# A decoder layer on eight cores: when the second feed-forward block is normalised, when three weights are loaded, and how buffer addresses are chosen

## The chip, the cores and the metric

The kernel runs on the 8 cores of one Trainium2 chip. Each core takes one sequence of the batch and runs the same program; nothing is exchanged between cores. The time of a run is that of the slowest core, in microseconds (us) of device time. Times inside the kernel come from one profiled execution, on core 1, the slowest one, unless another core is named.

## The reference, cut to what matters

```python
x = x + g1 * rmsnorm(concat([y_mla, y_ret]) @ w_out, post_norm_mix)      # (B, S, 1024)
h = rmsnorm(x, pre_norm_ffn) * (1.0 + sc2) + sh2
f = (jax.nn.silu(h @ w_gate) * (h @ w_up)) @ w_down                       # D_FF = 2816
x = x + g2 * rmsnorm(f, post_norm_ffn)
```

S is 4096. `y_mla` is causal softmax attention over 8 heads (query and key width 96, value width 64) and `y_ret` is a chunked retention over 4 heads; both come out of one input projection of a normalised `x`. The change touches the feed-forward part (the last three lines) and the place where it meets the attention part.

## The kernel before, in words

A core's 4096 tokens are cut into 8 blocks of 512. The program has three stages.

1. **Input projection and retention**, for token blocks 0 to 7 (about 100 to 455 us).
2. **Attention**, over query blocks in the order 6, 7, 5, 4, 3, 2, 1, 0 (`order`; about 480 to 1090 us). Per query block it runs score matmuls into banks of PSUM, the exponential on ACT (the tile `PT`), the causal mask on POOL for tiles on the diagonal, and `PT` times `V` on PE. Into these loops other work is mixed as "fill": the queries of the next block, and `outproj` of the block before (L1122). `outproj` has a part `pre` per 128 tokens (loads `yg` and the residual `xt`, transposes) and a part `proj`: 16 matmuls with `Wo`, copies to `mo`, bn statistics, one `-0.5` power on POOL, `xt + mo` on POOL, and a store of `xt` to a scratch in HBM (`x_scr` in the rows, `x1` in the code).
3. **Feed-forward**, over the same 8 blocks in the same order (L1370 on). For each block `prep2` (L1231) loads four tiles `xa` of 128 tokens from the scratch, squares them on ACT with a running sum, takes the power on POOL, scales them on DVE into `xn`, transposes them on PE and writes the result, scaled and shifted, to `h2T` on DVE. Then come 22 steps `jj`: 8 matmuls with a slice of `Wg`, 8 with one of `Wu`, SiLU on ACT into a tile `sgt`, and `up * sgt` on DVE into `h1T`. Then, for each of the four rows of 128 tokens (`j`), 2 x 22 matmuls with `Wd` into two banks, squares on ACT (`t`), the power on POOL, a scaling on DVE, `xb + t` on POOL and the store to `out`.

In the first feed-forward block (`si == 0`) the `outproj` of the last query block (`late`, L1373) is mixed between the steps `jj`, and at `jj == 10` stands `prep2` of the second block. In the later blocks `prep2` of the next block stands at `jj == 10` too.

The weights are read once, cast to bf16 on the way, by transfers issued on POOL: `Wg` and `Wu` in six groups each (five of 512 columns, the sixth of 256), `Wd` in six groups. `loads[si]` (L1224) names the groups whose transfers stand at the head of query block `si`; `tail_loads` (L1225) names those after the last query block; `Wd3` to `Wd5` stand at `jj == 9` of the first feed-forward block. Everything else is loaded and stored by SP.

**What sets the order.** `record` writes all operations down in program order with what they read and write. `_list_schedule` (L344) then lays them out per engine by a list schedule with modelled durations; where several operations are ready, the one written down first goes first. The result is a fixed order on each engine, and each engine works strictly in its order. A transfer is issued by its engine and lands later.

**What sets the addresses.** A first pass records the life of each buffer in program order; `_place` (L281) then gives each an address, and a buffer may lie where another lay before it. The new buffer's first writer waits then for the old one's last readers. `place` (L274) tries seeds (random changes in the order in which long-lived buffers are placed) and takes the first plan that fits.

Of the kernel before, what the change touches and what calls it, by code (L numbers as in the profile page):

```python
# [19 lines left out]
NSB = 8  # L20
# [142 lines left out]
class Sched:  # L163
    def __init__(self, plan=None):
        self.order = []
        self.plan = plan
        self.bufs = []
        self.arena = None
        self.nc = None

    def buf(self, name, cols, dt=F32, pin=False, fix=None):
        size = cols * (2 if dt == BF16 else 4)
        size = (size + 63) // 64 * 64
        b = Buf(name, size, "sb")
# [6 lines left out]
        if self.plan is not None:  # L181
            b.addr, b.over = self.plan[b.no]
        if self.plan is None:
            v = self.arena[:, 0:size // 4]
            if dt != F32:
                v = v.bitcast(dt)
            b.v = v[:, 0:cols]
        else:
            b.v = self.nc.alloc_sbuf_tensor_at(name, [128, cols], dt, offset=BASE + b.addr)[:, :]
# [84 lines left out]
    def place(self):  # L274
        for seed in range(200):
            plan = self._place(seed)
            if isinstance(plan, list):
                return plan
        raise RuntimeError(plan)

    def _place(self, seed):  # L281
# [8 lines left out]
        def cls(b):  # L290
            if b.pin or b.fix is not None:
                return -1 if b.fix is not None else 0
            return 1 if b.last - b.first > 1000 else 2

# [4 lines left out]
        for i, b in enumerate(order):  # L299
# [21 lines left out]
            best = None  # L321
            for lo, hi in holes:
# [9 lines left out]
                if best is None or sc < best:  # L332
                    best = sc
# [171 lines left out]
def record(nc, S, dr, arena, psum):  # L505
# [717 lines left out]

    loads = [[], [], [('g', 0), ('u', 0), ('g', 1)], [('u', 1)], [('g', 2), ('u', 2)], [('g', 3)], [], [('u', 3)]]  # L1224
    tail_loads = [('g', 4), ('u', 4), ('g', 5), ('u', 5), ('d', 0), ('d', 1), ('d', 2)]  # L1225

# [144 lines left out]
    for si, s in enumerate(order):  # L1371
        nxt = []
        late = outproj(order[-1], yms[NSB - 1]) if si == 0 else []  # L1373
        for jj in range(NJ):
# [15 lines left out]
            if si == 0 and jj == 9:  # L1390
                ffn_load([('d', 3), ('d', 4), ('d', 5)])
            if jj == 10 and si + 1 < NSB:
                for _ in prep2(order[si + 1], (0, 1) if si else (4, 5), nxt):
                    pass
        for j in range(4):
# [17 lines left out]
            for hf in range(2):  # L1413
                hs = slice(hf * 512, (hf + 1) * 512)
                stt(t_.v[:, hs], PS[fb[hf]], st.v[:, 2:3], G2b.v[:, hs], ALU.mult, ALU.mult, [PSB[fb[hf]], (st, 2), G2b], [(t_, hf)])
                tt("pool", xt.v[:, hs], xt.v[:, hs], t_.v[:, hs], ALU.add, [(xt, hf), (t_, hf)], [(xt, hf)])
            dma("sp", dr["out"][tb * 128:(tb + 1) * 128, :], xt.v, r=[xt], w=[(outD, tb)])
        h2T = nxt[0] if nxt else None
    OP("sp", lambda g: None, r=[outD])


def build_nc():
# [37 lines left out]
    with contextlib.ExitStack() as ctx:  # L1460
# [6 lines left out]
        record(nc, S0, dr, arena, psum)  # L1467
        S = Sched(S0.place())
        record(nc, S, dr, arena, psum)
# [97 lines left out]
```

How the kernel before makes its waits and increments, by code:

```python
    def then_inc(self, *a, **kw):  # L144
        return self
# [326 lines left out]
        def run(e, engobj):  # L472
            for op in self.ops[e]:
                for d in op.waits:
                    if d.is_dma:
                        n = NSEM[d.eng]
                        engobj.wait_ge(dsem[d.eng][d.dma_i % n], 16 * (d.dma_i // n + 1))
                    else:
                        engobj.wait_ge(esem[d.eng], d.count)
                ins = op.emit(engobj)
                if op.is_dma:
                    ins.then_inc(dsem[e][op.dma_i % NSEM[e]], 16)
                elif op.marked:
                    if ins is None:
                        ins = engobj.nop()
                    ins.then_inc(esem[e], 1)
```

## Time and profile before

| | us |
|---|---|
| median of three runs | 2189.97 |
| lowest and highest of them | 2080.72, 2330.53 |
| the profiled execution | 2075.85 |
| its span, from the first to the last instruction of core 1 | 2074.0 |
| spans of the eight cores | 2057.9 to 2074.0 |
| PE busy (matmul) | 1873.1 (90%) |
| DVE, ACT, POOL busy | 812.3, 959.3, 623.7 |
| read and written in HBM | 172 MB, 49 MB |

PE, DVE, ACT, POOL and SP are the engines; PEld is PE's loading of weights, which overlaps the matmuls. "bank" is a bank of PSUM. A number in square brackets at the end of a row of a timeline is how long the engine was idle before the row, and the name behind the arrow is what ended that wait. `x4` is the number of instructions merged in a row.

### The profile page before, as it was taken

The numbers are of one execution on the slowest core, as the hardware profiler recorded it, in microseconds if no ns is written. First come the engines' busy times: TensorE is split into PE (matmuls) and PEld (weight loads), VectorE is DVE, ScalarE is ACT, GpSimd is POOL, SyncE is SP. The second block draws the span as 40 slices with busy tenths as digits, with TensorE's granted clock in tenths as the row PEclk, the third lists the DMA queues.
The fourth block names the chain that finished last, engine by engine and source line by source line (L and its number), as shares of the span: only waits on it lengthen the run. The fifth ranks groups of instructions, "written<-read, shape, count | busy, mean of one in ns | idle before, by whom it ended". The sixth has DMA issues, their size and how long they took to land.

```text
span 2074.0 us, 39088 instructions; the slowest of 8 cores (2057.9 to 2074.0 us)
## 1 busy us (share of the span) xinstructions
PE 1873.1 (90%) x13536; PEld 973.7 (47%) x13536; DVE 812.3 (39%) x1739; ACT 959.3 (46%) x1485; POOL 623.7 (30%) x919
## 2 busy tenths in 40 slices
PE   0598999768889899999989799999999999999998
PEld 0255545434455555555544344444444444444443
DVE  3356556454354233456685422222131313122121
ACT  3466656528889999998851112121121212121111
POOL 3345456440243233335573411030201112020202
PEclk9999999988999999999999999999999999999999
DMA  7924445444333252354379812030201112030101
GB/s 227 190 60 128 124 122 130 122 82 148 86 111 95 61 104 85 83 126 115 106 181 176 216 42 82 21 102 11 91 30 63 53 51 72 21 102 21 51 21 62
DMA packets 94665, 195.51 MB, mean 94 GB/s; under 512 B 10376, under 2 KB 40584, under 8 KB 94472
## 3 DMA queue, kind: packets, MB, share of 16 engines
q1 hardware_dynamic: 65560, 162.79, 25.0%
q0 software_dynamic: 28912, 30.21, 10.0%
q8 instruction: 113, 1.85, 0.4%
q14 instruction: 80, 0.66, 0.1%
HBM read 172.32 MB, written 48.76 MB: 107 GB/s over the span
## 4 chain that ended last, share of the span: by engine, by line
PE 74%; DMA 8%; ACT 6%; issue 4%; SPq 3%; DVE 3%; POOL 2%; POOLq 0%; DVEq 0%; ACTq 0%
PE bank L542 72%; ACT PT L518 5%; SPq L515 3%; PE bank L549 2%; DMA W<-w 2%; DMA yg_scr<-yn 2%; DMA waf<-w_ada 1%; DMA x_scr<-xt 1%; DMA ckTb<-ck_scr 1%; DMA xa<-x_scr 1%; DVE Q L534 1%; DVE mo L529 1%; ACT yn L518 0%; DMA gp<-gpost 0%; POOL yn L521 0%
## 5 line engine op out<-in xcount | busy, mean ns | idle before, releaser
L518 ACT ACTIVATE PT<-bank 128x1024 bf16<-128x1024 f32 (+3 forms) x584 | 515.3, 944 | 75.7 <-PE bank L542 68.5
L542 PE MATMUL bank<-h2T,Wg 128*128 128x512 bf16 x1408 | 336.9, 383 | 14.3 <-ACT sgt L518 11.4
L542 PE MATMUL bank<-Q,KT 96*128 96x512 bf16 (+3 forms) x1152 | 319.9, 365 | 28.8 <-ACT PT L518 16.0
L542 PE MATMUL bank<-h2T,Wu 128*128 128x512 bf16 x1408 | 333.5, 380 | 2.0 <-DVE bag L1172 2.0
L518 ACT ACTIVATE sgt<-bank 128x512 bf16<-128x512 f32 x176 | 104.9, 597 | 477.7 <-PE bank L542 441.3
L542 PE MATMUL bank<-Wd,h1T 128*128 128x512 bf16 x1408 | 307.2, 379 | 0.0
L521 DVE TENSOR_TENSOR h1T<-bank,sgt 128x512 bf16<-128x512 f32 x176 | 121.5, 691 | 425.9 <-PE bank L542 415.9
L542 PE MATMUL bank<-W,hT 128*128 128x512 bf16 (+2 forms) x1280 | 259.6, 358 | 27.8 <-DMA W<-w 9.6
L542 PEld LDWEIGHTS bank<-V,PT 128*128 128x128 bf16 x4224 | 201.3, 97 | 124.5 <-issue 15.2
L542 PE MATMUL bank<-V,PT 128*128 128x65 bf16 x4224 | 222.4, 193 | 4.5 <-POOL PT L521 3.2
L542 PEld LDWEIGHTS bank<-h2T,Wg 128*128 128x128 bf16 x1408 | 138.1, 98 | 181.6 <-issue 20.5
L542 PEld LDWEIGHTS bank<-Wd,h1T 128*128 128x128 bf16 x1408 | 137.8, 98 | 166.1
L542 PEld LDWEIGHTS bank<-h2T,Wu 128*128 128x128 bf16 x1408 | 137.6, 98 | 166.6 <-issue 3.0
L521 POOL TENSOR_TENSOR st<-st 128x1 f32<-128x1 f32 x32 | 6.2, 193 | 644.8 <-ACT t L518 644.8
L542 PEld LDWEIGHTS bank<-W,hT 128*128 128x128 bf16 x1280 | 123.8, 100 | 144.3 <-issue 42.0
L518 ACT ACTIVATE t<-bank 128x512 f32<-128x512 f32 x64 | 38.1, 596 | 280.6 <-PE bank L542 240.7
L542 PE MATMUL bank<-Wo,yT 128*128 128x512 bf16 x512 | 155.6, 379 | 3.3 <-DVE bag L1172 1.9
L521 POOL TENSOR_TENSOR PT<-PT,trib 128x256 bf16<-128x256 bf16 x136 | 88.5, 670 | 220.4 <-ACT PT L518 219.9
L542 PEld LDWEIGHTS bank<-Q,KT 96*128 96x128 bf16 x1152 | 93.6, 97 | 112.9 <-issue 75.1
L529 DVE SCALAR_TENSOR_TENSOR t<-bank,st,G2b 128x512 f32<-128x512 f32 x64 | 45.1, 747 | 254.6 <-POOL st L521 254.6
L521 POOL TENSOR_TENSOR xt<-xt,mo 128x512 f32<-128x512 f32 x64 | 87.6, 1385 | 31.1 <-DVE mo L529 26.1
L521 POOL TENSOR_TENSOR xb<-xb,t 128x512 f32<-128x512 f32 x64 | 79.6, 1265 | 29.7 <-DVE t L529 29.3
(159 smaller groups left out, 1857.6 us busy)
## 6 DMA issues: line engine op xcount, KB each, us to landing
xt<-x SPq DMA_DIRECT2D x64, 512.0 KB, 5.4
x_scr<-xt SPq DMA_DIRECT2D x32, 512.0 KB, 2.7
xa<-x_scr SPq DMA_DIRECT2D x32, 512.0 KB, 6.2
xb<-x_scr SPq DMA_DIRECT2D x32, 512.0 KB, 3.3
out<-xb SPq DMA_DIRECT2D x32, 512.0 KB, 2.6
waf<-w_ada SPq DMA_DIRECT2D x4, 2048.0 KB, 22.6
wadab<-w_ada POOLq DMA_DIRECT2D x8, 1024.0 KB, 14.1
yg_scr<-yn SPq DMA_DIRECT2D x32, 256.0 KB, 3.3
```

The lines of the kernel that those rows point to most:

```text
L515: return OP(q, lambda g: g.dma_start(out=out, in_=in_), r, w, dma=True)
L518: return OP("act", lambda g: g.activation(out=out, in_=in_, func=func, **kw), r, w)
L521: return OP(eng, lambda g: g.tensor_tensor(out=out, in0=a, in1=b, op=op), r, w)
L529: return OP("dve", lambda g: g.scalar_tensor_tensor(out=out, in0=a, scalar=sc, in1=b, op0=op0, op1=op1), r, w)
L534: return OP(eng, lambda g: g.tensor_copy(out=out, in_=a), r, w)
L542: x = g.matmul(out, lhsT=l, rhs=rh, start=st, stop=sp, **kw)
L549: x = g.transpose(out=out, in_=i, identity=identb.v)
```

## The change

It has three parts.

- `prep2` of the second feed-forward block leaves `jj == 10` of the first block and is written behind the first row (`j == 0`) of that block's down projection. It takes banks 0 and 1 there for its transposes, where it took 4 and 5. The later blocks keep theirs.
- The transfers of `Wg5`, `Wu5` and `Wd0` are written at the head of the last query block and no longer behind it.
- Of the seeds, the first eight plans that fit are each recorded and laid out by the list schedule, and the one with the smallest modelled end is taken. The limit of life by which `_place` calls a buffer long-lived varies with the seed.

```diff
     def place(self):
-        for seed in range(200):
+        for seed in range(400):
             plan = self._place(seed)
             if isinstance(plan, list):
-                return plan
-        raise RuntimeError(plan)
+                yield plan
...
-            return 1 if b.last - b.first > 1000 else 2
+            return 1 if b.last - b.first > (1000, 500, 1500, 250)[seed % 4] else 2
...
-    loads = [[], [], [('g', 0), ('u', 0), ('g', 1)], [('u', 1)], [('g', 2), ('u', 2)], [('g', 3)], [], [('u', 3)]]
-    tail_loads = [('g', 4), ('u', 4), ('g', 5), ('u', 5), ('d', 0), ('d', 1), ('d', 2)]
+    loads = [[], [], [('g', 0), ('u', 0), ('g', 1)], [('u', 1)], [('g', 2), ('u', 2)], [('g', 3)], [], [('u', 3), ('g', 5), ('u', 5), ('d', 0)]]
+    tail_loads = [('g', 4), ('u', 4), ('d', 1), ('d', 2)]
...
-            if jj == 10 and si + 1 < NSB:
-                for _ in prep2(order[si + 1], (0, 1) if si else (4, 5), nxt):
+            if jj == 10 and 0 < si < NSB - 1:
+                for _ in prep2(order[si + 1], (0, 1), nxt):
                     pass
...
             dma("sp", dr["out"][tb * 128:(tb + 1) * 128, :], xt.v, r=[xt], w=[(outD, tb)])
+            if si == 0 and j == 0:
+                for _ in prep2(order[1], (0, 1), nxt):
+                    pass
...
-        S = Sched(S0.place())
+        best = None
+        for plan in itertools.islice(S0.place(), 8):
+            S = Sched(plan)
+            S.dry = True
+            record(nc, S, dr, arena, psum)
+            S.schedule()
+            if best is None or S.model_time < best[0]:
+                best = S.model_time, plan
+        S = Sched(best[1])
```

The numbers behind names in the following rows are those of the buffers, and line numbers after the change are one higher than before. ACT, in the first feed-forward block, before (`xn<-xa` are the squares of `prep2`, `t` those of the down projection):

```order
L518 ACTIVATE sgt<-bank 128x512 x9
L518 ACTIVATE xn_806,xst_928<-xa 128x1024
L518 ACTIVATE xn_806,xst_932<-xa 128x1024
L518 ACTIVATE xn_806,xst_934<-xa 128x1024
L518 ACTIVATE sgt<-bank 128x512 x3
L518 ACTIVATE xn_806,xst_930<-xa 128x1024
L518 ACTIVATE sgt<-bank 128x512 x9
L518 ACTIVATE t_948,st_947<-bank 128x512 x2
```

The same place after:

```order
L519 ACTIVATE sgt<-bank 128x512 x17
L519 ACTIVATE xn_806,xst_944<-xa 128x1024
L519 ACTIVATE sgt<-bank 128x512
L519 ACTIVATE xn_806,xst_942<-xa 128x1024
L519 ACTIVATE sgt<-bank 128x512
L519 ACTIVATE xn_806,xst_946<-xa 128x1024
L519 ACTIVATE sgt<-bank 128x512 x2
L519 ACTIVATE t_940,st_939<-bank 128x512 x2
L519 ACTIVATE t_951,st_950<-bank 128x512 x2
L519 ACTIVATE xn_806,xst_948<-xa 128x1024
```

The first square has moved from behind the 10th of the block's 22 SiLU to behind the 18th, and the fourth stands behind the squares of two rows of the down projection.

PE, the place of the transposes of the second block's `xn`, before (in the last steps `jj` of the first block):

```order
L542 MATMUL bank<-h2T_807,Wg_894 128x512 x8
L549 MATMUL bank<-identb,xn_806 128x128 x16
L542 MATMUL bank<-h2T_807,Wu_903 128x512 x8
L549 MATMUL bank<-identb,xn_806 128x128 x16
L542 MATMUL bank<-h2T_807,Wg_904 128x512 x8
```

and after (behind 130 of the 176 matmuls of the down projection; `Wd_906` is `Wd0`, `Wd_924` is `Wd4`, `Wd_925` is `Wd5`):

```order
L543 MATMUL bank<-Wd_923,h1T 128x512 x4
L543 MATMUL bank<-Wd_925,h1T 128x512 x2
L543 MATMUL bank<-Wd_924,h1T 128x512 x4
L550 MATMUL bank<-identb,xn_806 128x128 x16
L543 MATMUL bank<-Wd_925,h1T 128x512 x2
L543 MATMUL bank<-Wd_906,h1T 128x512 x4
L550 MATMUL bank<-identb,xn_806 128x128 x8
L543 MATMUL bank<-Wd_909,h1T 128x512 x4
L550 MATMUL bank<-identb,xn_806 128x128 x8
```

The 32 transposes have moved by some 210 matmuls (88 that stood between them and the down projection, and 130 of its own). The last lines show as well that the rows of the down projection are no longer worked off one by one on PE.

POOL, the issues of the last three `Wd` and what stands between them, before (`Wd_923`, `Wd_924`, `Wd_925` are `Wd3`, `Wd4`, `Wd5`):

```order
L515 DMA Wd_923<-wd 128x4x1024
L515 DMA Wd_924<-wd 128x4x1024
L521 TENSOR_TENSOR xt_868<-xt_868,mo_874 128x512 x2
L526 TENSOR_SCALAR xst_934<-xst_934 128x1
L521 TENSOR_TENSOR xst_934<-xst_934,mhalf 128x1
L521 TENSOR_TENSOR bag_879<-bag_879,e_890 128x1
L521 TENSOR_TENSOR bag_879<-bag_879,mhalf 128x1
L521 TENSOR_TENSOR xt_872<-xt_872,mo_877 128x512 x2
L515 DMA Wd_925<-wd 128x2x1024
```

and after:

```order
L516 DMA Wd_923<-wd 128x4x1024
L516 DMA Wd_925<-wd 128x2x1024
L522 TENSOR_TENSOR bag_879<-bag_879,e_890 128x1
L522 TENSOR_TENSOR bag_879<-bag_879,mhalf 128x1
L522 TENSOR_TENSOR xt_872<-xt_872,mo_877 128x512 x2
L527 TENSOR_SCALAR xst_944<-xst_944 128x1
L522 TENSOR_TENSOR xst_944<-xst_944,mhalf 128x1
L527 TENSOR_SCALAR xst_942<-xst_942 128x1
L522 TENSOR_TENSOR xst_942<-xst_942,mhalf 128x1
L527 TENSOR_SCALAR xst_946<-xst_946 128x1
L516 DMA Wd_924<-wd 128x4x1024
```

`Wd4` (four chunks) and `Wd5` (two) have changed places: in the new plan `Wd4` lies where `xt_872` and `mo_877` lay, so its transfer waits until the last store of `xt` to the scratch has landed.

## Rows read from the trace of the kernel before

**Rows 1.** Span and granted clock of the slowest core:

```profile
core 1: 2074.0 us, clock 0.978
```

**Rows 2.** Busy time by stage, core 1 (stretch, length, busy and count of each engine, clock, DMA):

```profile
100.00:455.00 355.00, 318.55 (x2318) 179.07 (x2317) 204.35 (x608) 207.73 (x437) 180.09 (x295) 0.98 0.43 110
455.00:480.00 25.00, 6.41 (x15) 1.51 (x14) 4.74 (x15) 6.73 (x12) 4.04 (x5) 0.50 0.84 204
480.00:1080.00 600.00, 552.29 (x6262) 330.15 (x6259) 301.10 (x623) 522.06 (x607) 223.03 (x299) 0.98 0.39 103
1080.00:1220.00 140.00, 120.07 (x622) 56.02 (x623) 71.73 (x139) 24.79 (x40) 48.38 (x63) 0.94 0.73 169
1220.00:2074.00 854.00, 845.12 (x4058) 388.82 (x4056) 190.43 (x290) 161.19 (x330) 131.78 (x208) 1.00 0.16 53
...
1190.00:1200.00 10.00, 6.69 (x31) 3.61 (x32) 4.54 (x8) 3.20 (x6) 0.74 (x2) 0.55 0.23 58
```

**Rows 3.** What PE waited for, 1082 to 1225 us, core 1 (total, times, longest):

```profile
PE bank L542 <- ACT sgt L518: 11.4, 2, 8.9
PE bank L542 <- DVE bag L1172: 3.9, 3, 2.0
PE bank L542 <- DVE h2T L526: 2.9, 1, 2.9
```

**Rows 4.** The same on core 7:

```profile
PE bank L542 <- ACT sgt L518: 14.9, 2, 11.9
```

**Rows 5.** Timeline of PE, end of the first feed-forward block's steps `jj` (start, length, what):

```profile
1170.04 1.89 PE L542 MATMUL bank<-h2T,Wg 128*128 128x512 bf16 x8 [2.46 <-ACT sgt L518]
1173.92 2.54 PE L542 MATMUL bank<-h2T,Wu 128*128 128x512 bf16 x8 [1.99 <-DVE bag L1172]
1176.25 2.97 PE L542 MATMUL bank<-h2T,Wg 128*128 128x512 bf16 x8
...
1193.31 3.57 PE L542 MATMUL bank<-h2T,Wg 128*128 128x512 bf16 x8 [8.91 <-ACT sgt L518]
1196.68 1.91 PE L549 MATMUL bank<-identb,xn 128*128 128x128 bf16 x16
...
1200.37 1.06 PE L549 MATMUL bank<-identb,xn 128*128 128x128 bf16 x16
...
1218.53 38.15 PE L542 MATMUL bank<-Wd,h1T 128*128 128x512 bf16 x176
```

**Rows 6.** Timeline of ACT at the same place:

```profile
1164.36 1.06 ACT L518 ACTIVATE xn<-xa 128x1024 bf16<-128x1024 f32 x1 [15.09 <-DMA xa<-x_scr]
...
1189.77 1.06 ACT L518 ACTIVATE xn<-xa 128x1024 bf16<-128x1024 f32 x1 [9.86 <-DMA xa<-x_scr]
...
1192.57 1.69 ACT L518 ACTIVATE sgt<-bank 128x512 bf16<-128x512 f32 x3 [1.65 <-DMA x_scr<-xt]
```

**Rows 7.** Chain of waits, the two last stores of `xt` (start, length until landed):

```profile
1173.32 9.62 DMA x_scr<-xt
...
1183.48 8.89 DMA x_scr<-xt
```

**Rows 8.** Timeline of POOL, the last residual addition:

```profile
1180.48 2.48 POOL L521 TENSOR_TENSOR xt<-xt,mo 128x512 f32<-128x512 f32 x2 [4.97 <-DMA xt<-x]
```

**Rows 9.** Tile `Wd`, issues and landing of its six transfers:

```profile
L515 POOL DMA_DIRECT2D Wd<-wd x6: 744/788/835, 1099.0 to 1183.6; - x6
...
DMA to landing us min/median/max: 9.2/19.7/37.1
```

**Rows 10.** Tile `Wu`, its three transfers between 700 and 1000 us:

```profile
DMA to landing us min/median/max: 9.5/11.4/11.9
```

**Rows 11.** Timeline of SP, the first store of the feed-forward output:

```profile
1234.30 0.34 SPq L515 DMA_DIRECT2D out<-xb  x1
```

**Rows 12.** Tile `xa` of the first feed-forward block's normalisation, 1030 to 1082 us:

```profile
DMA to landing us min/median/max: 4.1/4.1/5.4
```

**Rows 13.** Tile `xa` of the second block's normalisation, 1100 to 1220 us:

```profile
DMA to landing us min/median/max: 5.1/6.1/6.7
```

More of the change, by code:

```diff
@@ L2 @@
 import heapq
+import itertools
 import types
@@ L169, in __init__ @@
         self.nc = None
+        self.dry = False
     def buf(self, name, cols, dt=F32, pin=False, fix=None):
@@ L182, in buf @@
             b.addr, b.over = self.plan[b.no]
-        if self.plan is None:
+        if self.plan is None or self.dry:
             v = self.arena[:, 0:size // 4]
```

## The prediction, made before the changed kernel ran

> **What bounds the kernel now.** I read the busy time by stage first [rows 2]. From 1220 us on PE is busy 845.1 of 854 us: the feed-forward part is bound by PE, and the 8.9 us missing are the end of the last block. The input projection leaves PE idle for 355 - 318.6 = 36.4 us, the change to attention for 18.6 us of 25, attention for 600 - 552.3 = 47.7 us, and the stretch from 1080 to 1220 us, which holds the steps `jj` of the first feed-forward block, for 19.9 us. The reader is to see that the two written edits can act only in the last of these and just ahead of it: everything behind is full.
>
> The waits of PE in that stretch come next [rows 3]: 11.4 us for ACT's SiLU, in two waits; core 7 has the same with 14.9 us [rows 4], so it is no accident of one core. The timeline of PE gives the places [rows 5]: 2.46 us before 1170.04, 1.99 us before 1173.92, and 8.91 us before 1193.31. The timeline of ACT says why [rows 6]. ACT works in its order, and at 1149 us the next thing there is the square of a tile `xa` of `prep2`; ACT stands idle for 15.1 us until its load has landed, and the SiLU behind it stands too. The fourth square waits for a second time, 9.9 us, until 1189.77. Its load lies where a tile `xt` lay, whose store was issued at 1173.32 and took 9.62 us [rows 7]. The SiLU behind it waits another 1.65 us for the last store of `xt` (1183.48 + 8.89 = 1192.4), since its tile `sgt` lies on that buffer [rows 6, 7]. PE has three pairs of banks to run ahead in; they are used up, so it stands.
>
> **The change part by part.** All sums are against the profiled execution, 2075.85 us (span 2074.0 [rows 1] and 1.85 us around it). The lowest of the three runs shown is 4.9 us above it, their median 114 us; the number I give is on the scale of the profiled execution.
>
> *`prep2` moved behind the first row of the down projection.* What it takes away:
>
> - The wait of 8.91 us. In the new order the first 18 of the 22 SiLU stand ahead of any square, and in the new plan none of the last ones lies on a buffer whose store is late. I take all of it.
> - The wait of 2.46 us: ACT was held up by the third square. All of it.
> - The wait of 1.99 us: DVE came to the product for `h1T` late, behind copies and statistics of `outproj`, which stay. Between 0 and 1.99; I take 1.0.
> - The slow clock behind these gaps. The granted clock of 1190 to 1200 us is 0.55 [rows 2], that is, PE was for most of it on its level of 1.2 GHz in place of 2.4 GHz, after it had stood for 8.9 us. Eight matmuls take 1.89 us at the upper level and 2.54, 2.97 and 3.57 us behind the gaps, and 16 transposes 1.91 in place of 1.06 us [rows 5]: 0.65 + 1.08 + 1.68 + 0.85 = 4.3 us. I take it all.
>
> Together 8.9 + 2.5 + 1.0 + 4.3 = 16.7 us. The 32 transposes (2 x 0.89 us of PE) cost the same in either place. So the down projection, which began at 1218.5, should begin near 1218.5 - 16.7 - 1.8 = 1200.
>
> What it adds is a deadline in the down projection. Three of the loads of `xa` can go early, but the fourth lies on the tile `t` of the first row, and stands on SP behind that row's store to `out`. That store was issued 1234.30 - 1218.53 = 15.8 us after the down projection began, when the row's 44 matmuls ended at 9.5 us [rows 5, 11]. Now both halves of the row end after 48 matmuls (10.4 us at 0.217 us each, 38.15 / 176), so the store goes at 16.7 and the load at 17. It lands 4.1 to 6.7 us later [rows 12, 13], the square takes 1.06 us [rows 6], and I put 2 us on the two small steps on POOL and the scaling on DVE: ready at 24 to 27 us. The transposes stand behind 130 matmuls, at 28.2 us. Hidden, with 1 to 4 us to spare; where the load takes the 9.6 us of a slow transfer [rows 7], PE waits 2 us. Value 0, bounds 0 and 3. What covers it is the down projection itself.
>
> *The order of the last `Wd`.* `Wd4` now lies on the last `xt` and can be issued only when the store of it has landed, and it stands on POOL ahead of the statistics of `prep2`. The last `xt + mo` waited for its load until 1180.48 [rows 8], and its store was issued at 1183.48 and landed at 1192.4 [rows 7]. PE's last matmuls with `Wo` come about 5 us later in the new order (three groups of 8 stand in between), which the wait of 4.97 us for the load [rows 8] about swallows. So `Wd4` is issued near 1193. PE wants it after 36 matmuls of the down projection, at 1200 + 7.8 = 1207.8. A transfer of that size lands after 9.5 to 11.9 us where little else moves [rows 10], and six `Wd` took 9.2 to 37.1 us, median 19.7, when they were issued in a heap [rows 9]. That gives 1203 to 1213: between no wait and 5 us, with 2 or 3 us of slow clock on top. Only three tiles `xa` move beside it, so it is nearer to the first rows: I take 1.0, bounds 0 and 8.
>
> A page of the Trainium skill prices such a transfer: by "DMA: Bandwidth & Descriptors", Anatomy of one DMA, it takes about 2.0 us plus its bytes at 436 GB/s, an estimate of 4.4 us for the 1 MB written here. This trace has 9.5 us at the least for it, so the trace disagrees and decides; by the page this term would be 0 and the forecast 1 us lower.
>
> *`Wg5`, `Wu5` and `Wd0` released with the last query block.* PE waits for no weight in the stretch [rows 3], so an earlier landing gives nothing by itself. In the order of POOL two more transfers now stand between the masks of that query block: 0.8 us each [rows 9], 0 to 1.6, I take 1.0. They also share the DMA engines with the four loads of `xa` for the first block, at whose end PE already waits 2.9 us for `h2T` [rows 3]. The same loads took 4.1 us in the median there and 6.1 us where `Wd3` and `Wd4` were under way [rows 12, 13]: 2.0 us later at most for one load; I take 1.3.
>
> *The plan.* Other addresses give other waits in every stage. They remove no work. The idle time they can move is the 36.4, 18.6 and 47.7 us ahead of 1080 us [rows 2]; a tenth of these 103 us in either direction is what I allow. I take 0, bounds -10 and +10. That a plan is picked by modelled time is no price: the model holds fixed durations and no contention.
>
> **Sum.** -16.7 + 0 + 1.0 + 1.0 + 1.3 + 0 = -13.4 us. 2075.85 - 13.4 = 2062 us, 0.6% faster.
>
> **The rivals.**
>
> 1. *The stall moves to the new deadlines.* `Wd4` late by 5 us and slow clock (8 us), and the fourth `xa` late (3 us): 16.7 - 11 - 2.3 = 3 us gained, 2072 us. For it: the landing of up to 37 us [rows 9] and POOL standing in front of `Wd4`. Against it: few transfers are left at that time.
> 2. *The early weight transfers hold up the first normalisation: slower than before.* 3 MB are read in f32 and written as half of that in the 30 us in which the four `xa` of the first block, the residuals and `yg` come in. If a load of `xa` had to wait for the whole of them, PE would stand at its first feed-forward matmul for what they take: two of them at 9.5 to 11.9 us [rows 10] are 19 to 24 us, and 3 to 4 us of slow clock. At 2062 that is 2083 to 2089; I put it at 2085. It decides from a delay of 13.4 us on. Against it: `xa` beside two `Wd` under way took only 2 us longer [rows 12, 13].
> 3. *The plan gives more, or takes more, than the edits.* With a tenth of the idle time the sum ends at 2052 or at 2072.
> 4. *Nothing happens.* The new plan puts a late `sgt` or `xa` on a late buffer again and another wait of 8.9 us comes back: 2074 us.
>
> A rule of the skill bears on the second. "DMA: Bandwidth & Descriptors", SWDGE vs HWDGE vs iDMA, says that transfers issued from POOL and those issued from SP feed different queues inside each DMA engine, and that the engine takes turns between them. By that a load of `xa` is at most about doubled and never waits for a whole weight; the trace's step from 4.1 to 6.1 us agrees with it, and by it the rival could not reach its deciding point.
>
> **How the numbers follow.** The forecast's own case, 2056 to 2068 us, has 0.55. Rival 1 has 0.15, the plan's gain 0.10 (2046 to 2056), its loss 0.08 (2068 to 2078), nothing 0.07, the slower rival 0.05. The range is to hold 8 in 10: from 2049, which cuts off about half of the plan's gain, to 2076, which takes in rivals 1 and 4 and most of the plan's loss. A difference of 2%, some 41 us, is about what a measurement of this kernel can tell from no change. To be faster by that much the kernel would have to lose twice what the whole stretch from 1080 to 1220 us holds in idle time: 0.02. To be slower by it needs the second rival twice over: 0.03. Within it: 0.95.
>
> **What would show the steps right or wrong.** In the profile after: no wait of PE for `sgt` above 2 us between 1080 and 1220, and the down projection's first matmul at 1197 to 1204; a granted clock of 1.00 in the slices around it; `Wd4` landing before the 37th matmul of the down projection; the transposes with `xn` inside the down projection without a gap in front; PE's wait for `h2T` near 1082 us at 2.9 to 5 us; the stages up to 1080 us of the same length within 10 us. A gap of PE behind the first 36 matmuls with `Wd` would show rival 1; a gap of 10 us before the first matmul with `Wg` rival 2. The prediction would be wrong altogether if the projection or the attention stage changed by more than those 10 us.

## The result: 0.5% faster, and where the time went

The changed kernel takes 2073.62 us in the median of 20 runs (lowest 2064.64), the kernel before 2085.94 us in the median of its 20 (lowest 2078.25). The ratio is 0.9949, with a 95% interval of 0.9931 to 0.9967: about 10.6 us faster. That is inside the 2% called "no change". The profiled execution takes 2070.42 us. The two medians are over all 20 runs; the ratios and intervals of this document leave out the runs in which the cores of a die run at a lower clock, and without them the medians are about 2072 and 2083.5 us.

How to read the profile after: on core 1 the first matmul with `Wg` is at 1082.2 us, where it was at 1082.7 before, so that the two traces of this core can be laid side by side from there. Spans and clock of two cores (core 0 is the slowest now):

```profile
core 0: 2068.9 us, clock 0.977
core 1: 2058.9 us, clock 0.978
```

Busy time by stage, core 1 (stretch, length, busy and count of PE, PEld, DVE, ACT and POOL, granted clock, DMA share, GB/s):

```profile
100.00:455.00 355.00, 314.91 (x2259) 176.18 (x2258) 197.33 (x596) 203.77 (x428) 177.59 (x290) 0.95 0.42 105
480.00:1080.00 600.00, 548.09 (x6246) 325.74 (x6244) 301.59 (x621) 518.74 (x602) 223.41 (x298) 0.99 0.40 106
1080.00:1220.00 140.00, 134.32 (x691) 61.91 (x690) 69.43 (x133) 26.88 (x48) 50.38 (x66) 0.98 0.64 160
...
1060.00:1070.00 10.00, 7.78 (x49) 3.79 (x48) 7.71 (x21) 3.95 (x8) 9.78 (x17) 0.83 1.08 210
1070.00:1080.00 10.00, 6.09 (x62) 4.10 (x60) 10.00 (x20) 1.74 (x5) 6.21 (x9) 0.76 0.80 176
1080.00:1090.00 10.00, 8.33 (x57) 4.03 (x56) 5.60 (x12) 5.43 (x8) 6.07 (x8) 0.72 0.64 214
1190.00:1200.00 10.00, 10.00 (x48) 4.51 (x46) 3.46 (x5) 5.40 (x10) 3.04 (x7) 1.00 0.76 224
```

From 1080 to 1220 us PE is now idle for 140 - 134.3 = 5.7 us, against 19.9 [rows 2], and the slice from 1190 us is full at clock 1.00, where it had 0.55. The waits of PE from 1082 to 1225 us show no `sgt` at all any more (total, times, longest):

```profile
PE bank L543 <- DVE bag L1173: 1.9, 2, 1.2
PE bank L543 <- ACT PT L519: 1.3, 2, 0.9
PE bank L550 <- DVE mo L535: 1.0, 2, 0.5
PE bank L543 <- DVE mo L535: 0.8, 1, 0.8
```

The timeline of PE of core 1, through the down projection of the first block, has no gap before the 37th matmul or before the transposes; it is to be read beside [rows 5]:

```profile
1196.37 1.89 PE L543 MATMUL bank<-h2T,Wg 128*128 128x512 bf16 x8
1198.10 1.89 PE L543 MATMUL bank<-h2T,Wu 128*128 128x512 bf16 x8
1199.82 28.22 PE L543 MATMUL bank<-Wd,h1T 128*128 128x512 bf16 x130
1227.88 1.06 PE L550 MATMUL bank<-identb,xn 128*128 128x128 bf16 x16
1228.77 1.46 PE L543 MATMUL bank<-Wd,h1T 128*128 128x512 bf16 x6
```

**A table for all that follows.** The cores enter the feed-forward part 16 us apart before and 21 us apart in the changed kernel (29 in e7), and a single span hides a difference of 5 us. So I cut each core's trace at the same matmuls and average the lengths over the eight cores. "Projection" goes from the first projection matmul to the first `V` times `PT`; "q 6 to 2" is the first six query blocks; "last two" goes from the first `V` times `PT` of query block 1 to the first matmul with `Wg`; "q 1 to PE's end" from the same start to PE's last matmul, and "PE idle" is what PE stands still in it; "tail" is from there to the end of the span. The modelled end is the planner's. "Last two" does not hold the same matmuls in every kernel, since the list schedule also puts attention matmuls behind the first `Wg`: 494 before and in e1, 486 in the changed kernel, 498 in e12, 501 in e2, but 472 in e11 and 458 in e4 and e5 (all matmuls of PE in the stretch, core 1). So between e4, e5 or e11 and the others only the stretch to PE's end is a fair comparison. The stretches from query block 7 on repeat within about 1 us from core to core, save those with a late load in them. The projection does not: its mean was 417.8, 418.6 and 424.7 us in e1, e7 and e12, which have the same addresses there. (For e12 there were too few runs for a ratio.)

| kernel | modelled end | projection | q 6 to 2 | last two | q 1 to PE's end | PE idle | tail | ratio (95%) |
|---|---|---|---|---|---|---|---|---|
| before | 1992.5 | 417.1 | 540.3 | 59.2 | 1041.5 | 29.5 | 8.9 | 1 |
| changed | 1982.8 | 418.9 | 538.4 | 65.6 | 1031.9 | 19.0 | 10.7 | 0.9949 (0.9931 to 0.9967) |
| e1 move alone | 1982.7 | 417.8 | 540.4 | 59.0 | 1024.2 | 14.3 | 8.9 | 0.9932 (0.9903 to 0.9961) |
| e2 loads alone | 1996.1 | 412.2 | 541.2 | 62.6 | 1040.7 | 26.7 | 9.6 | 0.9965 (0.9938 to 0.9992) |
| e4 choice alone | 1990.2 | 418.8 | 540.4 | 58.8 | 1029.5 | 19.5 | 9.4 | 0.9968 (0.9944 to 0.9991) |
| e5 changed, three transfers held | 1983.0 | 415.8 | 538.9 | 61.8 | 1029.7 | 18.1 | 10.6 | 0.9918 (0.9887 to 0.9949) |
| e6 changed, fewer waits | 1982.8 | 416.1 | 537.0 | 65.0 | 1031.4 | 19.3 | 8.8 | 0.9906 (0.9879 to 0.9933) |
| e7 move, fewer waits | 1982.7 | 418.6 | 537.3 | 58.9 | 1024.2 | 14.7 | 8.8 | 0.9875 (0.9847 to 0.9902) |
| e8 both edits, first plan | 1988.7 | 412.6 | 539.5 | 62.9 | 1032.2 | 20.7 | 9.3 | 0.9945 (0.9894 to 0.9997) |
| e9 changed without the move | 1988.1 | 425.5 | 539.5 | 67.4 | 1039.2 | 24.4 | 10.8 | 0.9989 (0.9962 to 1.0016) |
| e10 changed, worst plan of eight | 2000.1 | 429.3 | 544.6 | 64.4 | 1036.4 | 23.8 | 9.5 | 1.0051 (1.0031 to 1.0070) |
| e11 as e7, best plan of 400 | 1979.0 | 412.5 | 540.2 | 66.3 | 1032.1 | 19.3 | 8.8 | 0.9912 (0.9890 to 0.9934) |
| e12 as e1, two more transfers | 1982.9 | 424.7 | 541.9 | 64.2 | 1030.9 | 18.6 | 8.9 | none |

From the first row to the second the mean span falls from 2067.5 to 2059.9 us, 7.6 us: the stretch of the steps `jj` (first `Wg` to first `Wd`) from 135.7 to 117.9 us, -17.8; what follows it +1.8, since the transposes have moved there; the last two query blocks **+6.4**; the tail **+1.8**; query blocks 6 to 2 -1.9, projection +1.8 and the start +0.2. So the stall was removed as forecast, and half of it was paid back in two places. Of the 6.4 us, 3.6 are idle time of PE (9.6 before, 13.2 after) and 2.7 are longer busy time (49.7 and 52.4) with 8 matmuls fewer, at a lower clock: 0.83, 0.76 and 0.72 in the slices from 1060 us on core 1, where before it was

```profile
1060.00:1070.00 10.00, 9.30 (x65) 4.13 (x62) 9.90 (x26) 4.97 (x10) 9.10 (x15) 1.00 0.87 170
1070.00:1080.00 10.00, 6.77 (x73) 4.07 (x72) 10.00 (x20) 3.05 (x6) 9.80 (x16) 1.00 0.73 203
1080.00:1090.00 10.00, 7.31 (x45) 3.61 (x46) 6.23 (x13) 3.70 (x5) 4.89 (x5) 0.83 0.76 236
```

The waits of PE in the last two query blocks of the changed kernel, 1017 to 1082 us on core 1, lie at `PT` and `mo`, and hardly at `h2T`:

```profile
PE bank L543 <- ACT PT L519: 4.5, 9, 1.3
PE bank L550 <- DVE mo L535: 2.2, 2, 1.5
...
PE bank L543 <- DVE mo L535: 1.1, 2, 0.9
...
PE bank L550 <- DVE h2T L527: 1.1, 1, 1.1
```

The 7.6 us are from one execution of each kernel; the runs say 10.6. The experiments ask who pays for the 6.4 us.

### The profile page after: what moved, and what is told of

Read it like the earlier page. It is cut to its first block, busy times and chain, and to the rows that moved or that the text cites. A ratio compares the mean times of both kernels' runs of the same rounds, so it can differ in the third digit from the quotient of the medians.

```text
span 2068.9 us, 39095 instructions; the slowest of 8 cores (2047.6 to 2068.9 us)
## 1 busy us (share of the span) xinstructions
PE 1875.2 (91%) x13536; PEld 970.5 (47%) x13536; DVE 814.9 (39%) x1739; ACT 959.2 (46%) x1485; POOL 620.1 (30%) x919
## 4 chain that ended last, share of the span: by engine, by line
PE 73%; DMA 9%; ACT 7%; issue 4%; DVE 3%; SPq 2%; POOL 1%; POOLq 0%; DVEq 0%; ACTq 0%
PE bank L543 71%; ACT PT L519 5%; DMA yg_scr<-yn 3%; PE bank L550 2%; SPq L516 2%; DMA W<-w 2%; DMA waf<-w_ada 1%; DMA ckTb<-ck_scr 1%; ACT yn L519 1%; DVE Q L535 1%; DMA xa<-x_scr 0%; DVE mo L530 0%; DMA kp_scr<-kpT 0%; DMA wstage<-wkv 0%; ACT xn L519 0%
## 5 line engine op out<-in xcount | busy, mean ns | idle before, releaser
L543 PE MATMUL bank<-W,hT 128*128 128x512 bf16 (+2 forms) x1280 | 263.4, 361 | 44.3 <-DVE r L522 14.3
```

The lines of the kernel that those rows point to most:

```text
L543: x = g.matmul(out, lhsT=l, rhs=rh, start=st, stop=sp, **kw)
```

## The experiments

**The two edits and the choice, one at a time.** The first theory (L) was that the early weight transfers cost the 6.4 us, the second (P) that the chosen addresses do. e1 is the move alone:

```diff
-            if jj == 10 and si + 1 < NSB:
-                for _ in prep2(order[si + 1], (0, 1) if si else (4, 5), nxt):
+            if jj == 10 and 0 < si < NSB - 1:
+                for _ in prep2(order[si + 1], (0, 1), nxt):
...
+            if si == 0 and j == 0:
+                for _ in prep2(order[1], (0, 1), nxt):
+                    pass
```

> Kernel before with one edit: prep2 of the second block behind the first row of the down projection. Loads and plan rule as before. Measured by the mean over the eight cores of four stretches of PE: last two query blocks (first V times PT of query block 1 to the first matmul with Wg: 59.2 us before, 65.6 after), steps jj of the first block (to the first matmul with Wd: 135.7 and 117.9), rest (to PE's end: 846.6 and 848.4), tail (to the span's end: 8.9 and 10.7). Both theories: steps jj 118 to 120, rest 848.4. Theory L (the early weight transfers cost the 6.4 us of the last two query blocks): they stay at 59.2, tail 8.9 to 10.7, ratio 0.992 or 0.993. Theory P (the chosen plan costs them): 59.2 as well, since this kernel has the plan of before. If they rise to 65 here, it is the moved prep2 itself that costs them, ratio 0.996.

It gained 17.3 us from query block 1 on and left the last two query blocks and the tail as they were. To PE's end it takes 7.7 us less than the changed kernel; the ratios, 0.9932 and 0.9949, lie the same way, but their intervals overlap. So the move does not cost anything; what was paid back comes with the other parts, loads and plan. The expectation calls this "the plan of before". That holds up to the steps `jj` of the first feed-forward block only: from there on e1's `sgt` and `xa` have other addresses, and no `sgt` lies on the last `xt` any more, where one did [rows 6, 7]. The 17.3 us are thus order and addresses together.

e2 is the other edit alone:

```diff
-    loads = [[], [], [('g', 0), ('u', 0), ('g', 1)], [('u', 1)], [('g', 2), ('u', 2)], [('g', 3)], [], [('u', 3)]]
-    tail_loads = [('g', 4), ('u', 4), ('g', 5), ('u', 5), ('d', 0), ('d', 1), ('d', 2)]
+    loads = [[], [], [('g', 0), ('u', 0), ('g', 1)], [('u', 1)], [('g', 2), ('u', 2)], [('g', 3)], [], [('u', 3), ('g', 5), ('u', 5), ('d', 0)]]
+    tail_loads = [('g', 4), ('u', 4), ('d', 1), ('d', 2)]
```

> Kernel before with one edit: Wg5, Wu5 and Wd0 at the head of the last query block (the first plan that fits is then another). Theory L: last two query blocks 64 to 66 us against 59.2, all else as before, ratio 1.003. Theory P: 59 to 60 us and ratio 1.000. Both: the steps jj of the first block stay near 135.7, since an earlier weight ends no wait there; below 131 would mean that the crowd of transfers had a part in the late loads of xa, and the move had less to take away.

The last two query blocks rose to 62.6 us (with 7 matmuls more in them), and the steps `jj` fell to 131.4. That is half of what L said, and the ratio, 0.9965, lies below both forecasts. The addresses moved with the edit, so this run alone decides nothing, and whether `jj` fell by the addresses or by a smaller crowd of transfers stays open.

e4 is the third part alone, the choice among eight plans on the program of before:

```diff
-        S = Sched(S0.place())
+        best = None
+        for plan in itertools.islice(S0.place(), 8):
...
+            if best is None or S.model_time < best[0]:
+                best = S.model_time, plan
+        S = Sched(best[1])
```

> Kernel before with the choice among eight plans alone (modelled end 1990.2 us against 1992.5). Theory L and P: no more than 3 us either way, steps jj 133 to 137, ratio 0.999 to 1.001. If plans matter as much as theory P needs, the stretches ahead of the feed-forward part should differ from before by some us in sum: last two query blocks outside 58 to 61.

This missed: the steps `jj` took 124.0 us against 135.7, and the stretch to PE's end fell by **12.0 us** with not one operation moved by hand. The timeline of ACT of core 1 says how (the squares of the second block, their `READ_ACCUMULATOR` rows left out):

```profile
1157.17 1.06 ACT L519 ACTIVATE xn<-xa 128x1024 bf16<-128x1024 f32 x1 [12.73 <-DMA xa<-x_scr]
...
1161.87 1.06 ACT L519 ACTIVATE xn<-xa 128x1024 bf16<-128x1024 f32 x1 [3.55 <-DMA xa<-x_scr]
...
1173.63 1.06 ACT L519 ACTIVATE xn<-xa 128x1024 bf16<-128x1024 f32 x1 [5.62 <-DMA xa<-x_scr]
...
1178.27 1.05 ACT L519 ACTIVATE xn<-xa 128x1024 bf16<-128x1024 f32 x1
```

ACT still waits 12.73 us in front of the first square, as it did before [rows 6], but the wait of 9.86 us for a tile on the last `xt` but one has become 5.62, and PE waits 0.9 us for `sgt` where it waited 11.4 [rows 3] (2.5 us on core 7, where it was 14.9 [rows 4]). In this plan none of the second block's four `xa` and none of the block's `sgt` lies on an `xt` of `outproj`, and no SiLU waits for a store of `xt` any more. A plan brings its own order as well: ACT has two squares ahead of the next SiLU here, and three before [rows 6]. Addresses and the order that follows from them made most of the stall, though `prep2` stood at the same place.

e9 asks the same from the other side, the changed kernel with the move undone:

```diff
-            if jj == 10 and 0 < si < NSB - 1:
-                for _ in prep2(order[si + 1], (0, 1), nxt):
+            if jj == 10 and si + 1 < NSB:
+                for _ in prep2(order[si + 1], (0, 1) if si else (4, 5), nxt):
```

> The changed kernel with prep2 of the second block back at jj == 10; early loads and choice among plans stay (seed 20 is chosen again, modelled end 1988.1 us). If the move is worth here what it was worth in the plan of before, from query block 1 to PE's end takes 1031.9 + 17.3 = 1049 us. If the plan's addresses take most of the stall away by themselves, as the choice alone did (1041.5 to 1029.5), the move is worth only some 5 us: 1035 to 1039, ratio 0.996 to 0.999. Last two query blocks 64 to 66 in either case; tail 10 to 11, with 23 waits ahead of the last reduction.

1039.2 us, so the move is worth 7.3 us beside the choice, just above the 1035 to 1039 expected, and 17.3 without it. The last two query blocks, at 67.4 us, lay outside the 64 to 66. Move and choice remove the same waits, and their gains do not add: 17.3 + 12.0 would be 29.3.

**Early transfers or addresses?** Written out with the three transfers recorded behind the last query block, but with the changed kernel's addresses, the program comes out with the same order of instructions on all five engines, so there is no run of it. The list schedule issues a transfer as soon as its buffer is free in the model, wherever it is written: the kernel before issues `Wg5` at 1045.1 us too. The edit to `loads` acts only through the addresses, by making three buffers live longer. To hold the transfers back I had to make them wait for something:

```diff
+    for a_, kw_ in held:            # Wg5, Wu5, Wd0
+        dma(*a_, r=[yms[NSB - 1]], **kw_)
```

> The changed kernel with its own addresses, but the transfers of Wg5, Wu5 and Wd0 made to wait for the last head of the last query block, so that they are issued about 1095 to 1110 us and not at 1047 to 1058 us. From the first V times PT of query block 1 to PE's end the changed kernel takes 1031.9 us (mean of the cores), the one with the move alone 1024.2. Theory L (the transfers and their issues in the last query blocks cost it): 1024 to 1027, last two query blocks 59 to 61 against 65.6. Theory P (addresses and the order that follows from them): 1030 to 1034, last two 64 to 66.

The stretch to PE's end fell by 2.2 us, to 1029.7, between the two forecasts and close to P's 1030. The last two query blocks fell by 3.8, to 61.8, but with 28 matmuls fewer in them. The addresses are the changed kernel's; the order is not: from about 1040 us on the list schedule laid out all five engines otherwise (modelled end 1983.0 against 1982.8). Then the opposite, in e12: the move alone, which keeps its addresses, with the contents of `Wu5` and `Wd0` read and cast a second time behind the sixth head of query block 1:

```diff
+                    if si == 6 and h == 5:
...
+                            dma("pool", dr["spare"][i_, :, 0:c_ * n_].rearrange("p (c n) -> p c n", c=c_), src, r=[(ym, 5)], w=[S.key("spare")])
```

> The move alone, with the addresses it had, and two transfers more: the contents of Wu5 and Wd0 are read and cast a second time in the last part of query block 1, into a scratch in HBM that nobody reads, so that four weight transfers are issued in the last two query blocks, as in the changed kernel, and not two. Taking the three out of the changed kernel's last query blocks gave 3.8 us there (65.6 to 61.8) and 2.2 us to PE's end. If the transfers cost by themselves: last two query blocks 62 to 63 against 59.0, and from query block 1 to PE's end 1026 to 1028 against 1024.2. If all of it is addresses and order: 59 to 60 and 1024 to 1025. If transfers were the whole difference to the changed kernel: 65 to 66 and 1032.

The last two query blocks took 64.2 us and the stretch to PE's end 1030.9: **+6.7 us with two transfers more** (0.5 MB and 1 MB written), more than L's number and nearly as much as the difference to the changed kernel. Two things keep this from being the price of the transfers. They end in HBM and not in the core's own memory. And though the addresses are those of e1, the order is not: ACT's is the same, but PE, DVE, POOL and SP have another one from about 1050 us on (modelled end 1982.9 against 1982.7). No run changes the transfers and leaves the order. The loads of `xa` from query block 1 to the first matmul with `Wg`, from issue to landing, in e1 on core 3:

```profile
DMA to landing us min/median/max: 3.2/3.4/4.8
```

in the changed kernel on cores 1 and 6:

```profile
DMA to landing us min/median/max: 4.7/6.5/8.1
```

```profile
DMA to landing us min/median/max: 5.1/6.0/10.1
```

and in e12 on core 3:

```profile
DMA to landing us min/median/max: 3.4/5.5/13.6
```

On cores 0, 1, 3 and 6 the longest is 5.0 to 5.4 us before, 4.5 to 5.3 in e1, 7.9 to 10.1 in the changed kernel and 10.0 to 13.6 in e12; the medians differ by less, 3.4 to 5.2 in e1 and 4.5 to 6.6 in the two others. ACT takes these squares in order among the exponentials of the query block, so one late load can hold up attention as well; the fourth square of e12, on core 3:

```profile
1074.81 1.06 ACT L518 ACTIVATE xn<-xa 128x1024 bf16<-128x1024 f32 x1 [4.95 <-DMA xa<-x_scr]
```

The Trainium skill says in "DMA: Bandwidth & Descriptors", SWDGE vs HWDGE vs iDMA, that the DMA engines take turns between the queues fed by POOL and by SP. I had drawn from it that a load of `xa` beside a weight is at most about doubled. e12, with the addresses of e1, does not agree: the longest load takes 10.0 to 13.6 us against 4.5 to 5.3, 1.9 to 2.8 times as long on these four cores, with up to three weight transfers in flight, and the measurement decides.

One weight transfer is enough for a long load, and it matters which of the two is issued first. The fourth load of `xa` stands next to the transfer of `Wu3` in e1 and e5 alike; in e1 it is issued 0.5 us ahead of it (core 1),

```profile
1055.94 0.32 SPq L515 DMA_DIRECT2D xa<-x_scr  x1
1056.49 0.96 POOL L515 DMA_DIRECT2D Wu<-wu  x1
```

and in e5 2.3 us behind it:

```profile
1053.65 0.97 POOL L517 DMA_DIRECT2D Wu<-wu  x1 [0.50 <-issue]
1055.98 0.32 SPq L517 DMA_DIRECT2D xa<-x_scr  x1
```

Ahead of `Wu3`, by 0.5 to 0.8 us, this load takes 3.2 to 5.4 us on the eight cores of before and of e1; behind it, by 2.3 to 2.5 us, 7.3 to 9.2 us on the eight cores of e4 and of e5. So the long load of e5 does not stand there without a weight: holding three transfers back left `Wu3` in front of it. Nor is the longest landing the price by itself. PE's idle time in the last two query blocks (mean of the cores) is 11.9 us in e4, where the longest landing is 7.7 to 8.3 us, 13.2 in the changed kernel with 7.9 to 10.1, and only 10.9 in e12 with 8.8 to 13.6; it is 9.6 before and 9.0 in e1.

What remains with the transfers held (1029.7 against 1024.2 of e1, 5.5 us) comes with the plan and its order. One difference is seen on SP. In the changed kernel it issues two loads of `xa` just ahead of the four of `yg` (timeline of SP, core 1):

```profile
1036.07 0.99 SPq L516 DMA_DIRECT2D xa<-x_scr  x2
1037.25 8.53 SPq L516 DMA_DIRECT2D yg<-yg_scr  x4
```

where e1 issues one:

```profile
1038.43 0.51 SPq L515 DMA_DIRECT2D xa<-x_scr  x1
1039.10 6.94 SPq L515 DMA_DIRECT2D yg<-yg_scr  x4
```

DVE waits for that `yg`, 5.05 us in the changed kernel and 2.39 us in e1, and has the copies `mo` behind it, for which PE waits (DVE, then PE of the changed kernel, core 1):

```profile
1044.17 1.10 DVE L526 TENSOR_SCALAR ygb<-yg,sv 128x512 bf16<-128x512 f32 x2 [5.05 <-DMA yg<-yg_scr]
```

```profile
1047.31 0.38 PE L550 MATMUL bank<-identb,ym 128*128 128x128 bf16 x4 [1.55 <-DVE mo L535]
```

The load of `yg` was issued before the first weight transfer of that stretch, at 1046.8 us, and e5 has a wait of 2.10 us at the same transposes, so this part does not need the weights. It is some 1.5 us. The kernel before has a wait of 4.00 us for `yg` there too, with 59.2 us for the last two query blocks, so the wait of DVE by itself explains little. How the 7.7 us between e1 and the changed kernel divide stays open: holding the transfers gives 2.2, adding them to the other plan costs 6.7, and 5.5 are left with them held, each time with another order of the engines mixed in.

**Does the modelled end order plans?** e3 and e8 are one kernel, the two diffs of e1 and e2 with the first plan that fits; of e3 only the ratio is used, 0.9933 (0.9898 to 0.9968).

> The changed kernel without the choice among plans: both edits, first plan that fits (modelled end 1988.7 us, that of the chosen plan 1982.8). Theory L: last two query blocks 65.6 as in the changed kernel, ratio 0.995 to 0.997. Theory P: they return to 59 to 61, tail 8.9, ratio 0.992. By the modelled times it would be 5.9 us slower than the changed kernel, 0.998.

> Both edits with the first plan that fits, once more for an undisturbed profile. Theory L and P as for e3_both_first_plan: from query block 1 to PE's end 1032 by L and 1024 to 1027 by P (modelled end 5.9 us later than with the chosen plan: 1038). Last two query blocks 62.6 if they are as with the early loads alone, 65.6 if as in the changed kernel; tail 9 to 9.6.

1032.2 us to PE's end: the plan modelled 5.9 us later than the chosen one took as long. It fell where my first rival had put the danger in the changed kernel: PE waited for a late `Wd` in the down projection on all eight cores, for 0.4 to 5.6 us. The waits of PE from 1180 to 1260 us on core 7:

```profile
PE bank L542 <- DMA Wd<-wd: 5.6, 1, 5.6
```

e10 takes the plan of the eight with the latest modelled end:

```diff
-        for plan in itertools.islice(S0.place(), 8):
+        for plan in itertools.islice(S0.place(), 4, 5):
```

> The changed kernel with the fifth of the eight plans, the one with the latest modelled end (2000.1 us against 1982.8). If modelled time orders plans on the chip, query block 6 to PE's end takes 10 to 20 us more than the 1570.3 of the changed kernel, ratio 1.000 to 1.004. If it doesn't (the first plan, modelled 5.9 us later, took 1571.7), within 4 us of it, ratio 0.994 to 0.997. Tail near 9.3, since only 3 waits stand ahead of the last reduction.

and e11, on the kernel e7 (below), the one with the earliest among 400 seeds:

```diff
-        for seed in range(200):
+        for seed in (41,):
```

> The move alone with fewer waits, as e7, with the plan of the earliest modelled end among 400 seeds (1979.0 us against 1982.7). If modelled time orders plans: query block 6 to PE's end 1558 against 1561.5 in e7, ratio 0.985 to 0.986. If it doesn't: 1558 to 1568, ratio 0.987 to 0.990. For the projection there is no forecast by the model: 412 to 419.

The worst plan is worse, as forecast: 544.6 + 1036.4 = 1581.0 us from query block 6 to PE's end, against 1570.3, 10.7 us for a modelled 17.3; with its projection it is 0.5% slower than before. The best plan is not best: 540.2 + 1032.1 = 1572.3 us against 1561.5 of e7, 10.8 us more for a modelled 3.7 less. That is outside both forecasts (1558, and 1558 to 1568). It too has `Wu5` issued in the last query blocks. In these comparisons the model was right about a plan 17.3 us worse; modelled differences of 2.3 (e4), 3.7 (e11) and 5.9 us (e8) said nothing about the measured ones, -12.0, +10.8 and +0.3 us.

**The tail.** It grew from 8.9 to 10.7 us on every core alike. The end of POOL's timeline in the changed kernel, core 1:

```profile
2050.40 0.19 POOL L522 TENSOR_TENSOR st<-st 128x1 f32<-128x1 f32 x1 [3.98 <-issue]
```

ACT's last square had ended at 2048.98 us. "Issue" means that the profile shows nothing that the engine waited for. In between the trace has 22 semaphore instructions of POOL, 61 ns apart, from 2049.02 to 2050.29 us: the tile `st` lies in this plan where 21 transfers once wrote or read, and POOL, which has never asked for them, now asks for each. All had landed long ago. e6 changes the bookkeeping alone: an engine that waits for an operation takes over what that operation's engine knew of transfers.

```diff
+                known_dma[e] |= d.dmas
                 for f in ENGS:
...
             op.waits = waits
+            op.dmas = frozenset(known_dma[e])
```

> The changed kernel, same addresses and same order on every engine; an engine leaves out the wait for a transfer that it knows to have landed through another engine's earlier wait (7263 waits become 6228; the last reduction on POOL has 1 in place of 22). If the 1.3 us before that reduction are the one-by-one working off of these waits, the tail falls from 10.7 to 9.3 to 9.5 us. Theory that such waits are free everywhere else: from query block 1 to PE's end 1031 to 1032 as before, ratio 0.994. Theory that they hold the engines up in the attention part as well: two to six us less ahead of the feed-forward part, ratio 0.991 to 0.993.

The tail is 8.8 us, less than the 9.3 to 9.5 expected, and the same reduction starts 0.15 us behind ACT's last row:

```profile
2047.71 0.19 ACT L521 ACTIVATION_READ_ACCUMULATOR t<-bank 128x1 f32 x1
```

```profile
2048.05 0.19 POOL L524 TENSOR_TENSOR st<-st 128x1 f32<-128x1 f32 x1 [2.98 <-ACT t L521]
```

So that is settled. e7 puts the thinner waits on the move alone:

> The move alone (as in e1_move) with the same thinning of waits (7256 become 6251). If waits are free but for the tail: as e1_move, from query block 1 to PE's end 1024, tail 8.9, ratio 0.992 to 0.993. If they also cost in the other stretches: ratio 0.988 to 0.991.

It is the fastest kernel of the study: 2058.66 us in the median, 0.9875 (0.9847 to 0.9902), 1.3% faster than before. In the profile the thinner waits give 3.1 us in query blocks 6 to 2 and nothing behind; the rest of the distance to e1 (0.9932, 0.9903 to 0.9961, from another round of runs; the two intervals all but meet) I do not claim for them.

## Why the prediction was right and wrong

The removal of the stall was forecast rightly. Two steps failed: the base of the sum ("on the scale of the profiled execution", 2075.85 us, where the runs are at about 2083.5), which is most of the error of the number 2062, and the price of the last two query blocks (1.0 + 1.3 us for the early transfers and 0 for the plan, where they took 6.4 us more).

- **What bounds the kernel, and the stall.** Right. The steps `jj` were forecast at 16.7 + 1.8 = 18.5 us less and measured 17.8 less; the down projection begins at 1199.82 us on core 1, forecast 1200. But of the two causes, order and address, I priced the order only. "I take 0" for the plan was put beside the sum as if the two were apart; e4 shows that the plan alone is worth 12.0 us of the same stall.
- **The slow clock, 4.3 us.** The size was off. PE's busy time from query block 1 on fell from 1012.0 to 1009.9 us in e1, 2.1 us, and its idle time by 15.2, where I had 12.4 for the waits: two errors that cancel, and that is luck. In the changed kernel the busy time is 1012.9 us: what the end of the steps `jj` gives back, the slower clock between 1060 and 1090 us takes.
- **The deadlines of the down projection.** The fourth `xa` was hidden, as forecast: loaded at 1217.23, squared at 1221.27, its transposes without a gap. `Wd4` cost 0 and not 1.0: it was issued at 1198.5 (forecast 1193) and landed 8.6 us later, half a microsecond ahead of its matmul at 1199.8 + 36 x 0.217 = 1207.6. It was right by little; in e8 a `Wd` is late.
- **The early transfers, 2.3 us, and the plan ahead of 1080 us, 0.** Together these are the term that failed: 6.4 us. I had looked for the delay at the first matmul with `Wg`, as a wait for `h2T` of 2.9 to 5 us. On core 1 that wait is gone (1.1 us for `h2T` in all of the last two query blocks), and PE stands inside attention and `outproj` instead, 4.5 us for `PT` and 3.3 for `mo` (3.6 and 0.2 before), at a slower clock. The price came from a wrong reading as well: I took 6.1 us for loads of `xa` "where `Wd3` and `Wd4` were under way" [rows 13], but three of those four had landed by 1168.18 us on core 1, and `Wd3` was issued at 1168.8. Only the fourth, 6.7 us, lay beside `Wd4`; and two of the three loads of [rows 12] had `Wg5` or `Wu3` beside them. So the step from 4.1 to 6.1 us was no measurement of the crowd, neither for the term nor for the rule of turns that I saw confirmed by it. How much of the 6.4 us is the transfers and how much the plan, the runs leave open.
- **The second rival.** It had a mechanism of this kind (weights hold up the first normalisation), but I let it begin only with a load that waits for whole transfers, and gave it 0.05 with a price of 23 us (2085 against 2062). Its sizes are off too: `Wg5` and `Wu5` have 256 columns and write 0.5 MB each, so the three transfers read 4 MB and write 2, not 3 and 1.5.
- **The tail.** Not in the sum: 1.8 us, from waits that a plan adds and that no modelled duration holds.
- **The plan in the other stages.** Within the 10 us allowed: -1.9 us in query blocks 6 to 2, +1.8 in the projection, which is inside its scatter.
- **The sum and its level.** In means over the cores of the two profiled executions the change is -7.6 us against a forecast of -13.4. Of the 5.8 us between, the last two query blocks are 4.1, the tail 1.8, the stall 0.7, the plan elsewhere 0.1, and `Wd4` takes 1.0 back. By the runs the miss is smaller: the ratio says -0.51%, about -10.6 us, the forecast was -0.65%. But the number 2062 was put on the scale of one profiled execution, 2075.85 us, and that is below each of the 20 runs of before (lowest 2078.25; in a later round two of 26 runs lay below it, the lowest at 2074.82). The same sum put on 2083.5 us would have been about 2070, against 2072 measured. Of the 10 us by which the forecast number is too low, some 8 are this base.

## What to carry to other kernels

When a planner gives buffers their addresses, every edit is two: what it says, and the new addresses. Separate them before crediting either, by running the edit in the old plan and the new plan without the edit, and look whether the order of the engines stayed the same too; a stall that is read from the trace may be an address, and then a mere change of seed can remove it. Before a landing time is taken as "alone" or "beside a weight", look up what was in flight: whether a load is issued just ahead of a big transfer or just behind it made 3.2 to 5.4 or 7.3 to 9.2 us of it here. Put a forecast in microseconds on the median of runs and not on one execution. And a planner that chooses by modelled time kept off the worst plan here, but its choice among the good ones told nothing; what its model lacks is the landing of loads in a crowd, and the number of waits.

## What the runs showed of the hardware that was not expected

- On POOL a wait costs 61 ns though it has long been fulfilled; 21 of them in a row cost 1.3 us on the path to the end (tail 10.7 against 8.8 us without them).
- A load of 512 KB issued by SP 0.5 to 0.8 us ahead of a weight transfer of 1 MB (written) took 3.2 to 5.4 us, and issued 2.3 to 2.5 us behind it 7.3 to 9.2 us, each on 16 core traces. With three in flight it took 8.8 to 13.6 us (e12, eight cores).
- Two weight transfers that nobody reads (0.5 and 1 MB written), with the changed order of the engines that came with them, cost a kernel on eight cores 6.7 us, though the DMA share of the attention stage is 0.39 on average [rows 2].
- One profiled execution of before took 2075.85 us, while the median of comparable runs is about 2083.5.
